# Four idle buffers hold weight tiles at the borders between products, and the next rows' first half is turned earlier

## The reference

```python
x = first_block(...)     # conditioning, dilated + gated linear attention, 32 experts, top 4
# second block
h = layer_norm(ALPHA * h + 0.5 * swiglu(h, ffn1_w1, ffn1_w3, ffn1_w2), ln1_g, ln1_b)       # "f1", then ln1
...                      # h @ w_in ("in2"), two attentions, gates
mix = (g_mla * (a @ w_up_mla) + g_diff * (b @ w_up_diff)) @ w_o    # "up_mla", "up_diff", "o2"
h = layer_norm(ALPHA * h + mix, ln2_g, ln2_b)
h = layer_norm(ALPHA * h + memory_attention(h, mem, w_q, w_kv, w_o), ln3_g, ln3_b)         # "mem_q", "mem_kv", "mem_o"
h = layer_norm(ALPHA * h + 0.5 * swiglu(h, ffn2_w1, ffn2_w3, ffn2_w2), ln4_g, ln4_b)       # "f2"
# third block
h = h + 0.5 * swiglu_3(rmsnorm(h, ffn1_norm), ffn1_w_gu, ffn1_w_down)                      # "f3"
u = rmsnorm(h, mix_norm);  ... u @ w_in ...                                                # "in3"
mixed = g_a * (out_a @ w_branch_dsa) + g_b * (out_b @ w_branch_moba)                       # "br_moba", "br_dsa"
h = h + mixed @ w_out                                                                      # "out3"
h = h + 0.5 * swiglu_3(rmsnorm(h, ffn2_norm), ffn2_w_gu, ffn2_w_down)                      # "f4"
```

## Time and profile before

| | |
|---|---|
| median of 3 runs | 2866.24 us (2865.05 to 2868.99) |
| the profiled execution, its own time | 2871.8 us |
| span of that execution | 2870.1 us |
| PE busy | 2729.5 us (95% of the span) |
| DVE busy | 2072.3 us (72%) |
| ACT busy | 1619.7 us (56%) |
| mean granted clock of TensorE | 0.975 of full speed |

### The profile page before, as it was taken

One profiled execution on the slowest core, in us unless ns is written; L12 is line 12 of the kernel. 1 busy time (PEld: TensorE's weight loads), 2 busy tenths in 40 slices (PEclk: granted clock), 3 DMA queues, 4 the chain that ended last, 5 costly groups with the idle time before them and its releaser, 6 DMA issues.

```text
span 2870.1 us, 38501 instructions
## 1 busy us (share of the span) xinstructions
PE 2729.5 (95%) x12256; PEld 2159.5 (75%) x12256; DVE 2072.3 (72%) x2458; ACT 1619.7 (56%) x2028; POOL 208.1 (7%) x212
## 2 busy tenths in 40 slices
PE   8997999999999999999969989899999899989999
PEld 5654888888888888888858877677787787867787
DVE  4555999999999999999954467765645545886644
ACT  2322888888888888888834434534343344345443
POOL 0001111111111111111100000000000000200000
PEclk9997999999999999999979999999999899999999
DMA  8745999999999999999946654253556455533554
GB/s 313 238 150 195 355 353 356 353 354 354 357 356 352 357 355 353 354 356 351 333 158 185 187 167 159 80 198 124 170 183 191 139 183 183 169 114 125 173 183 143
DMA packets 263623, 700.25 MB, mean 244 GB/s; under 512 B 29656, under 2 KB 128384, under 8 KB 213824
## 3 DMA queue, kind: packets, MB, share of 16 engines
q1 hardware_dynamic: 249780, 685.13, 67.8%
q0 software_dynamic: 9648, 8.42, 0.9%
q10 hardware_dynamic: 4124, 5.77, 0.6%
HBM read 706.51 MB, written 24.15 MB: 255 GB/s over the span
## 4 chain that ended last, share of the span: by engine, by line
PE 86%; DVE 7%; issue 2%; DMA 2%; ACT 2%; SPq 1%; POOL 0%; DVEq 0%; ACTq 0%; POOLq 0%
PE bank L584 23%; PE bank L586 23%; PE bank L585 23%; PE bank L1075 3%; PE bank L1074 3%; PE bank L1073 3%; PE bank L706 1%; PE bank L730 1%; DMA raw<-in_w_in 1%; PE bank L958 1%; PE bank L928 1%; PE bank L984 1%; DVE w_lo L1217 1%; PE bank L754 1%; PE bank L654 1%
## 5 line engine op out<-in xcount | busy, mean ns | idle before, releaser
L584 PE MATMUL bank<-w_hi,HTh 128*128 128x512 f32 (+1 forms) x2944 | 1189.1, 404 | 41.4 <-DVE HTl L1266 33.6
L586 PE MATMUL bank<-w_hi,HTl 128*128 128x512 f32 (+1 forms) x2944 | 1170.2, 397 | 0.0
L585 PE MATMUL bank<-w_lo,HTh 128*128 128x512 f32 (+1 forms) x2944 | 1169.5, 397 | 0.0
L1217 DVE TENSOR_TENSOR w_lo<-raw,w_hi 128x1024 fp32r<-128x1024 f32 (+1 forms) x444 | 528.5, 1214 | 295.6 <-ACT w_hi L2174 290.7
L2174 ACT ACTIVATE w_hi<-raw 128x1024 fp32r<-128x1024 f32 (+1 forms) x444 | 461.1, 1053 | 495.1 <-PE bank L586 329.6
L584 PEld LDWEIGHTS bank<-w_hi,HTh 128*128 128x128 f32 x2944 | 559.1, 190 | 182.2 <-DVE HTl L1266 40.3
L586 PEld LDWEIGHTS bank<-w_hi,HTl 128*128 128x128 f32 x2944 | 558.6, 190 | 133.4
L585 PEld LDWEIGHTS bank<-w_lo,HTh 128*128 128x128 f32 x2944 | 559.8, 190 | 121.5
L1854 DVE TENSOR_TENSOR w_lo<-arena,w_hi 128x1024 fp32r<-128x1024 f32 x256 | 315.8, 1234 | 45.7 <-ACT w_hi L2367 45.7
L1854 DVE TENSOR_TENSOR w_lo<-raw,w_hi 128x1024 fp32r<-128x1024 f32 x256 | 298.6, 1215 | 3.5 <-ACT w_hi L2412 2.0
L2367 ACT ACTIVATE w_hi<-raw 128x1024 fp32r<-128x1024 f32 x252 | 266.8, 1059 | 59.2 <-PE bank L586 59.2
(11 more groups left out here) (322 smaller groups left out, 2257.9 us busy)
## 6 DMA issues: line engine op xcount, KB each, us to landing
raw<-in_moe_w SPq DMA_DIRECT2D x128, 1024.0 KB, 4.9
arena<-in_moe_w SPq DMA_DIRECT2D x128, 1024.0 KB, 4.8
raw<-in_ffn_w SPq DMA_DIRECT2D x264, 256.0 KB, 3.4
H<-in_moe_w SPq DMA_DIRECT2D x64, 1024.0 KB, 4.8
MIX<-in_moe_w SPq DMA_DIRECT2D x64, 1024.0 KB
raw<-in_ffn_w_gu SPq DMA_DIRECT2D x176, 256.0 KB, 3.3
raw<-in_w_in SPq DMA_DIRECT2D x80, 512.0 KB, 4.7
raw<-in_ffn_w_down SPq DMA_DIRECT2D x88, 256.0 KB, 3.4
```

Of the source, the lines that this page charges most:

```text
L584: pe.matmul(acc, xh, wh, start=start, stop=False)
L585: pe.matmul(acc, xh, wl, start=False, stop=False)
L586: return pe.matmul(acc, xl, wh, start=False, stop=stop)
L1217: dve.tensor_tensor(w_lo[:, n % PARTS, 0:m], raw[:, n % RAW, 0:m], w_hi[:, n % PARTS, 0:m].bitcast(F32), ALU.subtract).then_inc(lo_done, 1)
```

## The change

Four buffers that are idle at the borders (`QT`, `KT`, `Y`, `MIX`, 8 KB a partition each) can each hold one tile's high and low part. They overlap in memory with tensors `extra0` to `extra3`; `Y` is moved behind `KT` so that the four lie side by side. A table `place_of` says for each tile where its parts go, and `freed_by` which tile must have been used before ACT may write there. `put_in` names the tiles at the borders: the last two down tiles of f1, f2, f3 and the first two of what follows; o2.0, o2.1, o2.6, o2.7, mem_q.2, mem_q.3 (mem_q.0 and .1 take the places of o2.2 and o2.3); the same in out3 and f4; mem_o.4 to .6 and f2.3.

With the places, the lows are given earlier on DVE. At the end of "up_diff", "o2", "mem_o", "br_dsa" and "out3" the two first lows of the next product stand before the evictions of the last block but one, and at "o2", "mem_o" and "out3" two more before the first half's eviction (`inside=PARTS`). At the end of f1, f2, f3 four lows of the next product instead of two stand before the first half's eviction. The lows within the norms go. In five products PE turns the first half's rows inside its last tile, three matmuls before the end. DVE then writes their lows (`rows_half(0)`) ahead of the second half's eviction; at the end of f1 and f3 the same lows stand between the two banks of the second half, with PE's turn where it was.

```diff
-        Y = sb("Y", [P, TT, D])
         H = sb("H", [P, TT, D])
+        with ExitStack() as shared:
+            EXTRA = [shared.enter_context(nc.sbuf_tensor(f"extra{i}", [P, 2 * TILE], F32R)) for i in range(4)]
         QT = sb("QT", [P, KD, S])
         KT = sb("KT", [P, KD, S])
+        Y = sb("Y", [P, TT, D])
...
+        place_of = {}
+        free_after = {}
+
+        def put_in(name, i, place, after=None):
+            n = (FFN[name].n0 if name in FFN else G[name][0].tiles[0].n) + i
+            place_of[n] = place
+            if after is not None:
+                free_after[n] = after
+
+        def first_of(name):
+            return FFN[name].n0 if name in FFN else G[name][0].tiles[0].n
+
+        IN_QT, IN_KT, IN_Y, IN_MIX = range(PARTS, PARTS + 4)
+        DOWN_LAST = 4 + FFN_TILES * (FFN_STEPS - 1)
+        for name, after in (("f1", "in2"), ("f2", "f3"), ("f3", "in3")):
+            put_in(name, DOWN_LAST, IN_QT, first_of(name))
+            put_in(name, DOWN_LAST + 1, IN_KT, first_of(name))
+            put_in(after, 0, IN_Y, first_of(name))
+            put_in(after, 1, IN_MIX, first_of(name))
+        for pair, up, wide, after in (("up_mla", "up_diff", "o2", "mem_q"), ("br_moba", "br_dsa", "out3", "f4")):
+            u = [(first_of(up) + i) % PARTS for i in range(4)]
+            put_in(wide, 0, IN_QT, first_of(pair))
+            put_in(wide, 1, IN_KT, first_of(pair))
+            for i in range(4):
+                put_in(wide, 2 + i, u[i])
+            put_in(wide, 6, IN_Y, first_of(wide))
+            put_in(wide, 7, IN_MIX, first_of(wide))
+            ring = [first_of(after) % PARTS, (first_of(after) + 1) % PARTS]
+            put_in(after, 0, ring[0])
+            put_in(after, 1, ring[1])
+            put_in(after, 2, IN_QT)
+            put_in(after, 3, IN_KT)
+        put_in("mem_o", 4, IN_QT, first_of("mem_kv"))
+        put_in("mem_o", 5, IN_KT, first_of("mem_kv"))
+        put_in("mem_o", 6, IN_Y, first_of("mem_kv"))
+        put_in("f2", 3, IN_MIX, first_of("mem_o"))
+        user = {}
+        freed_by = []
+        for t in tiles:
+            place = place_of.setdefault(t.n, t.n % PARTS)
+            freed_by.append(max(user.get(place, -1), free_after.get(t.n, -1)) + 1)
+            user[place] = t.n
...
+        def hi_at(n, c):
+            i = place_of[n]
+            return w_hi[:, i, c] if i < PARTS else EXTRA[i - PARTS][:, c]
+
+        def lo_at(n, c):
+            i = place_of[n]
+            return w_lo[:, i, c] if i < PARTS else EXTRA[i - PARTS][:, c.start + TILE:c.stop + TILE]
...
+                                    if not lead and tail and tt == 1 and t is b.tiles[-1] and j == t.kts - 1:
+                                        turned_early.append(turn_half(*tail, 0))
...
-            gemm("up_diff", kt0=4, tail=True)
-            gemm("o2", rows_of=(MIX, "gated2"), tail=True)
+            gemm("up_diff", kt0=4, tail=(MIX, "gated2"))
+            gemm("o2", rows_of=(MIX, "gated2"), tail=(X, "ln2"))
             gemm("mem_q", rows_of=(X, "ln2"))
...
+                            if inside and b is G[name][-1]:
+                                rows_half(0)
...
-                    split_to(b.tiles[-1].n + 1)
+                    split_to(b.tiles[-1].n + (3 if inside and b is G[name][-1] else 1))
                     if last is not None:
                         read(last)
                     last = b
-                if tail is None:
-                    ahead(last.tiles[-1].n + 1, more)
+                if tail is None or inside:
+                    ahead(last.tiles[-1].n + 1, inside or more)
...
                 def tail(tt, nxt):
 
                     k = centre(n, tt)
-                    if tt == 0:
-                        split_to(nxt + 1)
-                        spread(n, tt, k)
-                        signal(f"ln{n}")
-                    else:
-                        rows_half(0)
-                        split_to(nxt + 2)
-                        spread(n, tt, k)
-                        signal(f"ln{n}")
+                    spread(n, tt, k)
+                    signal(f"ln{n}")
+                    if tt == 1:
                         vec_over(f"ln{n}_g")
                         vec_over(f"ln{n}_b")
-                        split_to(nxt + 4)
                         rows_half(1)
                 return tail
 
@@ -1420,18 +1477,10 @@
...
-                split_to(min(n + 4, len(tiles)))
+                split_to(min(n + 2 + PARTS, len(tiles)))
...
+                        if rows_inside and tt == 1 and i == 0:
+                            rows_half(0)
...
-            lead(first_tile("o2"))
-            gemm("o2", onto_x(1.0), tail=layer_norm(2))
+            lead(first_tile("o2"), True)
+            gemm("o2", onto_x(1.0), tail=layer_norm(2), inside=PARTS)
...
-                    high(i, tiles[i].landed, i - PARTS + 1 if i >= PARTS else None)
+                    high(i, tiles[i].landed, freed_by[i] if freed_by[i] else None)
...
-                split_to(min(n + 2 + PARTS - 1, len(tiles)))
+                split_to(min(n + 2 + PARTS, len(tiles)))
...
-            gemm("up_mla", "up_diff", hold=1)
+            gemm("up_mla", "up_diff")
             lead(first_tile("o2"))
-            gemm("o2", hold=1)
+            gemm("o2")
             lead(first_tile("mem_q"))
```

76 lines of the change are left out of this document (35 added, 41 removed).

## The result

The changed kernel takes 2879.36 us (median of 5 runs, 2874.34 to 2882.03), before 2866.24; the ratio is 1.004, with a 95% interval from 1.0027 to 1.0053, or 8 to 15 us more. The forecast was 2872.8 us and slower, the range 2861 to 2880.

What follows compares the result with a forecast made beforehand. PE, busy 95% of the span, was taken to idle at borders, nearly always waiting for DVE. Terms -0.6 + 2.2 + 0.2 + 5.8 + 3.1 - 4.1 = +6.6 us on 2866.2 gave 2872.8 us, range 2861 to 2880.

Steps and rivals of the forecast that it cites:

- f1, f2, f3: Ends of f1, f2, f3: a low waiting for its load delays the first eviction; -0.6, +2.2 and +0.2 us.
- "up_diff" to "o2", "br_dsa" to "out3": Earlier turn and row lows let "o2" and "out3" start sooner: -2.3 us at each.
- further -1.7 us at "out3": With 2.3 us of idle gone, the slow clock behind 2642.03 goes too: eight matmuls at 0.23 instead of 0.43 us.
- "o2" to "mem_q": Late mem_q loads and four lows hold evictions; PE waits 8.7 us in the last tile; +5.8 us with the border before.
- One of my signs of being wrong: End of "o2": the prediction is wrong if mem_q's loads land by 1875; mem_q.0 was forecast at about 1881.5.
- The other sign: The prediction is wrong if DVE reaches the first half's eviction in "mem_o" before 2015.
- rival (b): mem_q.0's load overtakes the queue, changing only "mem_q" to -4 to +1 us: sum -3 to +2, some 2866 us; chance 0.10.
- "mem_o" to f2: Lows ahead hold the evictions; the turn waits 4.6 us, f2 starts at 2025.4 instead of 2023.40: +3.1 us.
- Two lows to 2013.1: In "mem_o": after mem_o.7's low, DVE makes two lows until 2013.1, then the first block's evictions until 2016.0.
- (a): The lows ahead fit into DVE's idle time and no eviction is held: -8.7 us, 2857.5 us; chance 0.15.
- (c): Three waits inside last tiles each bring an unhidden 1.2 GHz stretch, 1.7 us each: +11.7 us, 2878 us; chance 0.13.
- (d): Evictions are held, but less, with mem_q.0 two us sooner: +2 to +4 us, 2869 us; chance 0.17.

Runs made afterwards that it cites:

- second pair: Changed kernel and kernel before each run and profiled once more, unaltered: 2877.82 us (ratio 1.0029) and 2871.02 us (ratio 1.0004).
- run 8: "one ahead" with DVE's row lows of the first half again behind the second half's eviction, early turn kept: 2874.45 us, ratio 1.0012.
- Run 1: Changed kernel with only two lows ahead of the first eviction at the ends of f1, f2, f3, the others in the norm: 2868.77 us, ratio 0.9997.
- Run 4: Changed kernel with PE's turn of the first half again after the product's last matmul: 2885.54 us, ratio 1.0055.
- Run 3: Changed kernel with the memory rows' and bias's loads moved behind mem_q's tiles on SyncE's queue: 2874.55 us, ratio 1.0018.
- run 2: Changed kernel with the next product's lows back in the norm for up_diff, o2, mem_o, br_dsa, out3; early turn kept: 2875.84 us, ratio 1.0024.
- run 9: "one ahead" without the four extra places, every tile in the ring of four: 2890.16 us, ratio 1.0074.
- one ahead: Changed kernel, one low before first half's eviction in o2, mem_o, out3, two at f1 to f3 ends, memory loads behind mem_q's: 2857.63 us, ratio 0.9961.
- run 7: "one ahead" with PE's turn again after the product's last matmul: 2865.02 us, ratio 0.998.

## Why the prediction was right

The direction and the chain of causes were right, the size less so. The measured median, 2879.36 us, lies 0.6 us inside the upper end of the range and outside the 2868 to 2878 us that I gave as the forecast's own; the difference between the medians, 13.1 us, is twice the 6.6 us forecast.

In the table's stretches, forecast (summed from the terms) and measured (changed kernel less before, in the first profiles, in the second ones, and the mean of the two):

| stretch | forecast | first pair | second pair | mean |
|---|---|---|---|---|
| f1 to in2 | -0.6 | -0.5 | 0.0 | -0.2 |
| in2 to o2 | -2.3 | -3.9 | -1.4 | -2.7 |
| o2 to mem_q | +8.1 (the two together +5.8) | +6.6 | +7.9 | +7.3 |
| mem_o to f2 | +3.1 | +4.7 | +5.7 | +5.2 |
| f2 to f3 | +2.2 | +2.0 | +2.5 | +2.3 |
| f3 to in3 | +0.2 | +0.6 | 0.0 | +0.3 |
| in3 to out3 | -4.0 | -2.5 | -5.5 | -4.0 |
| out3 to f4 | -0.1 | -0.1 | +0.8 | +0.4 |
| mem_q to mem_o and f4 to the end, which the change doesn't touch | 0 | +1.4 | -1.8 | -0.2 |
| all | +6.6 | +8.4 | +8.4 | +8.4 |

Single stretches of the two pairs differ by up to 3 us, so a mean that agrees to 0.1 us, as at in3 to out3, is partly luck, and so is the same 8.4 in both pairs. With half of the low-clock time taken off, as in run 8, the pairs give +9.1 and +5.8 us.

**f1, f2, f3.** The low that waits for its load holds the first eviction: counted from the last turn inside f1, the eviction comes at 8.2 us instead of 6.2, 2.0 us late where 2.4 were forecast. At f2 nothing is taken back: the turn waits 13.74 us for 11.37. Run 1 takes the lows away and all three delays go.

**"up_diff" to "o2", "br_dsa" to "out3".** The wait of the first matmul falls by 2.3 us at each, as forecast. The further -1.7 us at "out3", for the low clock behind its wait, has no such ground. The second profile of before waits 2.62 us there too, and has the high clock behind it (first the first profile, then the second, from the first matmul of "out3" to its second turn):

```profile
2642.03:2646.48 4.45, 4.45 (x13) 3.48 (x14) 2.81 (x3) 0.00 (x0) 0.00 (x0) 0.62 0.63 223
```

```profile
2638.76:2641.66 2.90, 2.90 (x13) 2.32 (x14) 2.82 (x3) 0.00 (x0) 0.00 (x0) 1.00 0.56 194
```

So that term is in the one profile that I had, and not in the kernel. Run 4 gives the early turn's share at "o2", 0.65 us of the 2.3.

**"o2" to "mem_q".** In the forecast's own times "o2" starts at 1863.95; in the trace at 1858.14, 5.8 us lower. With that taken off, the forecast has mem_q.0 landing near 1875.7, the first half ready at 1889.7, the turn's wait 8.7 us and the second turn at 1898.3. The trace has 1874.9, 1888.5, 7.8 us and 1896.8. So the chain was right link by link, and a little too long. One of my signs of being wrong, mem_q's loads landing by 1875, was met as I had written it, in absolute time. It is not met on the forecast's scale: of the 5.8 us, 3.8 arose ahead of f1 and most of the rest in in2>o2, and counted from the second turn of "o2" the forecast had the load at 14.6 us (1881.5 less 1866.9), the trace at 13.9. The other sign did not come: DVE reaches the first half's eviction in "mem_o" at 2019.28. The queue filled as the forecast had it:

```profile
raw<-in_mem_w_q SPq DMA_DIRECT2D x6, 512.0 KB, 9.1
H<-in_mem SPq DMA_DIRECT2D x1, 1024.0 KB, 6.0
...
VEC<-in_ln_b SPq DMA_DIRECT2D x1, 512.0 KB, 10.0
```

These are the DMA issues from 1860 to 1880 us of the changed kernel (KB each, us to landing). ln_b is issued at 1863.5 and lands at 1873.5, mem_q.0 at 1864.9 and 1874.8: in the order of issue, so rival (b) falls. The Trainium skill ("DMA: Bandwidth & Descriptors", Queues, rings and completion order) allows another order; no run here shows one. Run 3 then shows that the load was worth 4.5 us of the wait, and four lows with the load in time 3.3.

**"mem_o" to f2** is the term that was mis-sized: +3.1 forecast, +5.2 measured (+4.7 in the first pair of profiles). The step of the forecast "Two lows to 2013.1" takes the loads of f2 as landed. In the trace ACT waits 1.58 us for f2.1, its low starts at 2012.96 and ends at 2014.2, 1.1 us later than forecast. The turn, which waited 5.9 us and not 4.6, takes the slow 1.97 us, where the one before took 1.09. The forecast counted a slow turn at mem_q and none here: from the start of the turn to the second half's eviction it has 2.8 us, the trace 3.3. These two make 1.6 us, the excess in the first pair. In the second pair before's own border is 1.2 us shorter, without its 3.4 us of low clock.

**"out3" to f4**: the wait of the turn was 1.5 us by the forecast and is 1.72 and 1.46 us.

**The rivals.** (a), all fits into idle time, is refuted by the rows of "o2" and "mem_o". (c), the clock costs more, holds at its borders and not in the sum. The stretches o2>mem_q and mem_o>f2 have 3.4 to 10.2 us more at the low clock than before, but much of it lies while PE waits, where it costs nothing (o2>mem_q takes 35.8 us with 6.8 us and 35.9 with 10.2). In the sum the changed kernel has 59 and 65 us at the low clock from f1 on, before has 60 and 60. (d), 2 to 4 us, is below the 8.4 measured.

**The gap to the median.** The first result is +13.1 us between medians, the second comparison 1.0029, or +8.3 us, and both pairs of profiles +8.4. The traces place the 8.4 by stretches. It is at the lower end of what the first set of runs gives (8 to 15 us); the rest of that set's difference is not explained.

## What to carry to other kernels

Work that is "made ahead" is only free in a wait. Ahead of the instruction for which the bottleneck engine waits, each piece costs its full length, and more if it itself waits for a load; so count how many fit between the last ready event and the next (here one or two lows, not four), and put the rest where that engine waits for its partner. Moving one instruction ahead moves everything that stood there behind: after the early row lows, the second tile's low became the next wait (run 2), and only both placements together gave 0.35 to 0.4%. Extra buffers may bring no gain in one order of the work, as here in the changed kernel, and still be what a better order needs (run 9). No run has them with the order of the kernel before.

## What the runs showed of the hardware

The granted clock is not a property of the kernel alone. Two profiles of one kernel differ by 3.4 us of low clock at the same place in the program, and the kernel before takes 5.3 us more ahead of the last turn of f1 in one profile than in the other, with the same work and a mean granted clock of 0.97 and 0.98. The Trainium skill ("TensorE: Matmul & The Clock Gate", What's actually happening) says of the slow matmuls at the start that their number is "run-variable"; these profiles show the same in the midst of a kernel.

How long PE waits at a border goes with the clock behind it, but not strictly. In run 8 the first matmuls of "o2", mem_q, f2, "out3" and f4 wait 3.53, 3.90, 3.86, 3.54 and 2.80 us, and the granted clock over the next 4 to 5 us is 0.68, 0.50, 0.64, 0.64 and 0.62 (the 1.2 GHz level for much or all of it); in "one ahead" they wait 0.3 us each, and it is 1.00 behind all five. In the kernel before they wait 2.6 to 2.8 us: in the first profile the low clock stands behind four of the five (0.62 to 0.67), in the second behind none. So an estimate that prices waits alone can come out too low, as mine did in runs 8 and 9, and one that prices a low stretch seen once can come out too high.

Most turns (eight transposes) take 1.03 to 1.09 us. All 25 turns at the borders that stand behind a wait of 3.27 us or more for DVE take 1.97 us, and so does one in run 7 behind 2.33 us, with a granted clock of 0.50; one in run 9 behind 3.07 us takes 1.09.
